# Half of the input rows and the memory tokens arrive already turned instead of being turned on TensorE

## The reference, cut to what matters

```
rmsnorm(x, g) = x * rsqrt(mean(x * x, axis=-1) + 1e-6) * g
h    = rmsnorm(x, norm_mix_g)                 # (2048, 1024)
proj = h @ w_in                               # q, k, v, pool and memory queries: 1792 columns
mkv  = rmsnorm(mem, norm_mem_g) @ w_mem_kv    # 256 memory rows
gates = sigmoid(h @ w_gate + b_gate)          # 3072 columns
merged = gates[0]*(y_attn @ Wa) + gates[1]*(y_pool @ Wp) + gates[2]*(y_mem @ Wm)
x = x + merged @ w_out
x = x + relu(rmsnorm(x, norm_mlp_g) @ w_up)**2 @ w_down
out = rmsnorm(x, norm_final_g)
```

## Time and profile before

| | us |
|---|---|
| median of three runs | 2591.36 |
| the profiled execution's own time | 2593.32 |
| its span in the trace | 2591.5 |
| TensorE busy | 2565.0 |
| VectorE busy | 1734.6 |
| ScalarE busy | 1157.6 |
| GpSimd busy | 551.3 |

### The profile page before, as it was taken

How to read it: one execution, slowest core, us unless ns; L and a number is a source line. 1 busy time by engine, 2 the same in 40 slices (tenths; PEclk the granted TensorE clock), 3 DMA queues, 4 the chain that set the end, 5 groups by cost and what they waited for, 6 DMA issues and landing times.

```text
span 2591.5 us, 33051 instructions
## 1 busy us (share of the span) xinstructions
PE 2565.0 (99%) x12065; PEld 2128.1 (82%) x12065; DVE 1734.6 (67%) x2401; ACT 1157.6 (45%) x2131; POOL 551.3 (21%) x510
## 2 busy tenths in 40 slices
PE   8999999999999999999999999999999999999998
PEld 7888888888887887888887888888888888888887
DVE  7778657666466655658778666765557566575886
ACT  6344535344344433434456455654555243342533
POOL 1455200000022152336554333000000112111100
PEclk9999999999999999999999999999999999999999
DMA  4778555666446787787797666633355585767753
GB/s 146 253 241 258 199 183 179 186 216 225 144 136 240 236 258 256 230 276 260 231 298 230 229 220 197 218 110 118 110 172 162 114 221 109 185 150 161 201 179 114
DMA packets 346764, 508.71 MB, mean 196 GB/s; under 512 B 33208, under 2 KB 213484, under 8 KB 346604
## 3 DMA queue, kind: packets, MB, share of 16 engines
q1 hardware_dynamic: 318956, 431.08, 51.5%
q0 software_dynamic: 27648, 75.51, 11.8%
HBM read 325.12 MB, written 181.40 MB: 195 GB/s over the span
## 4 chain that ended last, share of the span: by engine, by line
PE 93%; DVE 4%; issue 1%; ACT 1%; DMA 1%; POOL 0%; SPq 0%; POOLq 0%; DVEq 0%
PE ps L2416 29%; PE ps L2418 29%; PE ps L2417 29%; PE ps L2421 2%; PE ps L2693 1%; PE ps L2670 1%; PE ps L2438 1%; DVE res_lo L1653 1%; DVE s_lo L1647 1%; PE ps L2593 1%; PE ps L2621 1%; DMA res_raw<-in_w_down 0%; DMA proj_d<-c 0%; ACT scores L1123 0%; DVE res_lo L1641 0%
## 5 line engine op out<-in xcount | busy, mean ns | idle before, releaser
L2416 PE MATMUL ps<-res_hi,s_hi 128*128 128x512 f32 x3084 | 1204.3, 391 | 6.4 <-issue 1.7
L2418 PE MATMUL ps<-res_hi,s_lo 128*128 128x512 f32 x3084 | 1200.9, 389 | 0.0
L2417 PE MATMUL ps<-res_lo,s_hi 128*128 128x512 f32 x3084 | 1200.9, 389 | 0.0
L2416 PEld LDWEIGHTS ps<-res_hi,s_hi 128*128 128x128 f32 x3084 | 579.1, 188 | 130.0 <-issue 6.1
L2418 PEld LDWEIGHTS ps<-res_hi,s_lo 128*128 128x128 f32 x3084 | 579.0, 188 | 120.7
L2417 PEld LDWEIGHTS ps<-res_lo,s_hi 128*128 128x128 f32 x3084 | 579.2, 188 | 118.1
L1123 ACT ACTIVATE s_hi<-piece_f 128x512 fp32r<-128x512 f32 x436 | 274.3, 631 | 478.6 <-PE ps L2418 420.6
L1123 ACT ACTIVATE s_hi<-s_sum 128x512 fp32r<-128x512 f32 x327 | 204.1, 628 | 367.5 <-PE ps L2418 338.6
L1647 DVE TENSOR_TENSOR s_lo<-piece_f,s_hi 128x512 fp32r<-128x512 f32 x432 | 322.6, 747 | 34.5 <-ACT s_hi L1123 26.5
L1647 DVE TENSOR_TENSOR s_lo<-s_sum,s_hi 128x512 fp32r<-128x512 f32 x327 | 247.8, 758 | 87.9 <-ACT s_hi L1123 87.7
L1707 DVE TENSOR_TENSOR u<-u,ps 128x512 f32<-128x512 f32 x109 | 74.8, 686 | 294.5 <-PE ps L2418 294.4
(11 more groups left out here) (195 smaller groups left out, 2501.7 us busy)
## 6 DMA issues: line engine op xcount, KB each, us to landing
proj_d<-c SPq DMA_DIRECT2D x152, 256.0 KB, 3.3
piece_f<-in_w_up SPq DMA_DIRECT2D x32, 1024.0 KB, 6.8
up_d<-c SPq DMA_DIRECT2D x128, 256.0 KB, 3.3
piece_f<-up_d SPq DMA_DIRECT2D x32, 1024.0 KB, 7.0
piece_f<-in_w_gate SPq DMA_DIRECT2D x24, 1024.0 KB, 7.1
w_hi<-parts_d SPq DMA_DIRECT2D x48, 512.0 KB, 3.7
w_lo<-parts_d SPq DMA_DIRECT2D x48, 512.0 KB, 5.2
temp<-proj_d SPq DMA_DIRECT2D x48, 512.0 KB, 6.8
```

The lines of the kernel that those rows point to most:

```text
L2416: mm(dst, wh, xh, start=first, stop=False, skip_group_check=joins)
L2417: mm(dst, wh, xl, start=False, stop=False, skip_group_check=joins)
L2418: return mm(dst, wl, xh, start=False, stop=last, skip_group_check=joins)
```

## The change

The host gives two more inputs: the second half of x and the memory rows, laid out turned. For the five portions, TensorE's transposes and VectorE's products with the gain go away. In their place SyncE loads the turned portion into `ht` (1 MB, iteration N), ScalarE multiplies by the gain in two halves of four ACTIVATEs of 128x256 (iteration N+1), SyncE stores the 256 row factors to DRAM and loads them back, broadcast to all partitions, as `r_bc`, and GpSimd multiplies `ht` by them in four TENSOR_TENSORs (end of iteration N+1). Both halves of `ht` are stored in iteration N+2, before C22. The untouched rows are still loaded, for the sums of squares. Some semaphores are merged, with counts to match.

```diff
...
+            def load_turned(n):
+
+                if n not in NORM_AT:
                     return
...
+                if across(n):
+                    sp.wait_ge(hs_st, 64 * summed(n))
+                    for r in range(2):
+                        sp.wait_ge(ht_st[r], 16 * across(n))
+                else:
+                    sp.wait_ge(r_lo_done, PROD)
+                frm = a["mem_turned"] if n == MEM_AT else a["x_turned"][NORM_AT.index(n)]
+                sp.dma_start(ht[:], frm).then_inc(xt_ld, 16)
+
+            def store_factors(n):
...
+                sp.wait_ge(rs_pow, normed(n) + 1)
+                if across(n):
+                    sp.wait_ge(r_ld, 16 * across(n))
+                sp.dma_start(r_d[:], rrs[:]).then_inc(r_st, 16)
+
+            def load_factors(n):
...
+                sp.wait_ge(r_st, 16 * (across(n) + 1))
+                if across(n):
+                    sp.wait_ge(ht_done, 2 * across(n))
+                sp.dma_start(r_bc[:].rearrange("p n i -> p (n i)"),
+                             r_d.rearrange("n i -> (n i)").rearrange("(o n) -> o n", o=1).broadcast_to([P, 2 * P])).then_inc(r_ld, 16)
+
+            def store_turned(n):
...
+                sp.wait_ge(ht_done, 2 * across(n) + 2)
+                for r in range(2):
+                    if n == MEM_AT:
+                        sp.dma_start(mt_v[:, :, r * P:(r + 1) * P], ht[:, r]).then_inc(ht_st[r], 16)
+                    else:
+                        store_across(ha_v, n, r)
...
+                    load_turned(n)
                     if 0 <= n - SPLIT_AT < PARTS:
...
                         if across(n + 1):
-                            sp.wait_ge(xt_rdy, 2 * across(n + 1))
+                            sp.wait_ge(rs_sum, 4 * normed(n + 1))
                         load_rows(n + 1)
...
+                    store_factors(n - 1)
+                    store_turned(n - 2)
                     store_tile(n, 0, C22, 1, 1)
...
                     store_tile(n, 1, C11, 0, 0)
+                    load_factors(n - 1)
...
+            def turned_weighted(n, half):
+
+                if n not in NORM_AT:
+                    return
+                act.wait_ge(xt_ld, 16 * (across(n) + 1))
+                g0 = PM_MEM if n == MEM_AT else PM_MIX
+                for k in range(4 * half, 4 * half + 4):
+                    last = op(ht[:, :, k, :], ht[:, :, k, :], ACT.Copy, scale=par[:, g0 + k:g0 + k + 1])
+                last.then_inc(xn_done, 1)
...
             def norm_tiles(n):
 
-                if not hosts(n):
+                if not out_job(n):
...
                         norm_tiles(n - 1)
+                    turned_weighted(n - 1, 0)
                     if more:
                         s_split(n + 1, 2)
...
                         s_split(n + 1, 3)
+                    turned_weighted(n - 1, 1)
                     finish(n, C11, 2)
...
             def take_ht(n, r):
-                if not hosts(n):
+                if not out_job(n):
...
+                if n in NORM_AT and across(n) or n == IN_END:
+                    pool.wait_ge(r_st, 16 * across(n))
                 g_.tensor_tensor(rrs[:], rvar[:], m_half[:, 0:2], ALU.pow).then_inc(rs_pow, 1)
+
+            def turned_scaled(n):
...
+                pool.wait_ge(xn_done, 2 * across(n) + 2)
+                pool.wait_ge(r_ld, 16 * (across(n) + 1))
+                for r in range(2):
+                    by_row = r_bc[:, :, r].rearrange("p (o n) -> p o n", o=1).broadcast_to([P, 4, P])
+                    for h in range(2):
+                        half_row = ht[:, r, 4 * h:4 * h + 4, :]
+                        last = g_.tensor_tensor(half_row, half_row, by_row, ALU.mult)
+                    last.then_inc(ht_done, 1)
...
                         weight_sums(SUMS_AT.index(n))
+                    turned_scaled(n - 1)
...
             def rows_across(n, r):
 
-                if not hosts(n):
+                if not out_job(n):
...
```

More of the change, by code:

```diff
@@ L164, in across, with crossed @@
     return count(hosts, n)
+def crossed(n):
+    return count(out_job, n)
 def summed(n):
@@ L318, in build @@
     t1_raw = there("t1_raw", [P, 4, TB], 120)
+    r_bc = there("r_bc", [P, P, 2], 126)
     b21_raw = there("b21_raw", [P, 4, TB], 188)
@@ L394, in build @@
     setup = sem("setup")
-    ident_rdy = sem("ident_rdy")
     par_rdy = sem("par_rdy")
@@ L488, in build @@
     with_gain = sem("with_gain")
-    gf_ld = sem("gf_ld")
+    xt_ld = sem("xt_ld")
+    r_st = sem("r_st")
+    r_ld = sem("r_ld")
     def kp(w):
@@ L764, in store_tile, with store_across @@
                 sp.dma_start(to[r0:r0 + P, c0:c0 + TB], c_tile(n, which)[:]).then_inc(up_st[s], 16)
[L766 to L768 removed]
+            def load_turned(n):
+                if n not in NORM_AT:
                     return
[L770 to L774 removed]
+                if across(n):
[8 more added lines that the diff above has]
+                if n not in NORM_AT:
+                    return
+                sp.wait_ge(rs_pow, normed(n) + 1)
[3 more added lines that the diff above has]
+            def load_factors(n):
+                if n not in NORM_AT:
+                    return
[5 more added lines that the diff above has]
+            def store_turned(n):
+                if n not in NORM_AT:
+                    return
+                sp.wait_ge(ht_done, 2 * across(n) + 2)
[4 more added lines that the diff above has]
+                        store_across(ha_v, n, r)
+            def store_across(to, n, r):
+                t0 = t_at(n, r)
                 if r == 0:
@@ L778, in store_ht @@
                     sp.dma_start(to[:, 4:8, t0:t0 + P], ht[:, 1, 4:8, :]).then_inc(ht_st[1], 16)
+            def store_ht(n, r):
+                if not out_job(n):
+                    return
+                sp.wait_ge(ht_done, 2 * across(n) + r + 1)
+                store_across(ht_v, n, r)
             def store_sums(n):
@@ L2469, in rows_across @@
             def rows_across(n, r):
-                if not hosts(n):
+                if not out_job(n):
                     return
                 pe.wait_ge(xn_done, 2 * across(n) + r + 1)
-                if 2 * across(n) + r:
+                if 2 * crossed(n) + r:
                     pe.wait_ge(ht_done, 2 * across(n) + r)
@@ L2554, in pool_rows_across @@
                     last = transpose(ps[:, 6, g * P:(g + 1) * P], wp_st[:, g, :])
-                last.then_inc(wp_tr, 1)
+                last.then_inc(misc_done, 1)
             def fuse_pool(u):
@@ L2805 @@
         aps[name] = nc.dram_tensor(f"in_{name}", arrays[f"in_{name}"].shape, F32, kind="ExternalInput").ap()
+    x, mem = inputs["x"][0], inputs["mem"][0]
+    turned = {"x_turned": x[SEQ // 2:].reshape(2, 4, P, KT, P).transpose(1, 4, 0, 3, 2),
+              "mem_turned": mem.reshape(2, P, KT, P).transpose(3, 0, 2, 1)}
+    for name, laid in turned.items():
+        arrays[f"in_{name}"] = np.ascontiguousarray(laid)
+        aps[name] = nc.dram_tensor(f"in_{name}", arrays[f"in_{name}"].shape, F32, kind="ExternalInput").ap()
     out = nc.dram_tensor("out", (1, SEQ, D), F32, kind="ExternalOutput").ap()
```

39 lines of the change are left out of this document (19 added, 20 removed).

## The result

The changed kernel takes **2606.99 us** (median of 6 runs, 2601.70 to 2611.61); the kernel before, on the same chip, 2591.07 (2589.86 to 2592.15, 6 runs). The ratio is 1.0061, 95% interval 1.0044 to 1.0078: slower by 15.9 us, where the forecast was 2582.5 us, 8.9 less than before. The profiled execution took 2610.12 us, with a span of 2608.3.

A forecast was written before the change was run, and what follows sets the result against it. TensorE was taken to bound the kernel, busy 99% of the span and waiting for nobody from 70 to 345 us. Removed transposes gave -8.9, all else zero: 2591.36 to 2582.5 us, range 2580.7 to 2587.0.

The forecast's parts named there:

- What was removed: TensorE, input stage: ten groups of eight transposes at 0.89 us a group leave the chain, 8.9 us.
- the rival with 2569.6: TensorE: each of 80 transposes counts in full at 0.272 us, 21.8 us saved; chance 1%.
- What ScalarE and VectorE get: ScalarE: eight ACTIVATEs at 0.40, 3.2 us a portion, hidden by idle time; VectorE: loses 13.6 us off the path.
- VectorE is held up: VectorE stands still beside GpSimd's 25.9 us of new products, ending 12.3 us behind; at TensorE's cost 2594.8 us; chance 3%.
- The price of the parts on GpSimd and SyncE: GpSimd: 1.295 us a product, 5.2 a portion; SyncE: fifteen issues of 0.34 us, factor store and load landing in 4 each.
- the broadcast product is dear: GpSimd's product with a broadcast operand: slower by over 5.2 us from 3.7 us each, 2600.2 at 4.0; chance 5%.
- the tightest place: After portion 10, SyncE holds C22 and C11 for GpSimd; 6.9 and 6.5 us of slack remain, at worst 1.2 lost.
- the DMA queues are late: Loads for portions 4, 7, 10 each delay GpSimd's chain 4.6 us; TensorE waits 7.3 beside pieces 13, 14: 2589.8; chance 9%.
- where the queues were emptier: Argument against the late-queues rival: the turned loads come right behind the piece load, when DMA queues had less to do.
- the zero: The sum's entry for everything except the removed transposes: no gain and no loss counted.

The follow-up runs named there:

- the run with rests: Changed kernel with GpSimd's ten weight-sum sets spread over pieces 2 to 15 instead of 2 to 11: 2582.36 us, ratio 0.9966.
- the control without the change: Kernel before, with its weight sums spread over pieces 2 to 15 in the same way: 2591.30 us, ratio 1.0001.
- order-only kernel: Changed kernel with SyncE's factor, scaled-portion and block-sum transfers moved behind the store of C21: median 2600.37 us, ratio 1.0024; profiled again 2585.05.

## Why the prediction was wrong, point by point

**What was removed: right.** 8.9 us for ten groups; the run with rests is 8.7 under the kernel before, the control without the change 0.3 over it. A transpose costs the chain the distance of starts, not its 272 ns: the rival with 2569.6 would have asked for 22 us in the run where nothing waits. The page "TensorE: Matmul & The Clock Gate" of the Trainium skill (Part 4) gives about 275 ns for such a transpose in one kernel, in a sentence on bf16; the 272 ns of an fp32 one here agree with it as the length of one, not as its price.

**What ScalarE and VectorE get: right in the place, ScalarE's size too small.** Eight ACTIVATEs of 495 ns are 3.96 us a portion, over the 3.2 taken and the upper bound of 3.8, and they cost nothing; the wait for the turned load was 0.4 us. The rival "VectorE is held up" shows in one row, the s_lo of 5.18 us beside the scaling of portion 7; but VectorE then waited 7.29 us for the landing all the same, and the products alone in the kernel before cost no time (2591.23).

**The price of the parts on GpSimd and SyncE: right.** A product with the repeated operand takes 1.31 us (1.295 was taken), so the rival on the other side, "the broadcast product is dear", had the right sign for a wrong reason. The 8-byte store landed in 4.1 to 6.8 us, the broadcast load in 4.2 to 6.7, inside the bounds.

**The step that failed is the tightest place**, in two terms. First, the slip of the DMA queues was entered once, as one load of 1.05 MB at 230 GB/s, 4.6 us at portion 10. I took all other landings from the kernel before. But GpSimd's sets are a chain through some twenty landings, and every later one can slip: by the tenth set it was 34 us, not 4.6. Second, the end of scaling portion 10, put at 284.6, came at 314.75, and with it everything that SyncE held. The place itself was named rightly: C22 of piece 12, held behind the finished portion, stops S4 of piece 13, and that is the second wait, 8.0 us. What was not priced at all is the same place at portion 7, where the first and longest wait is (11.2 us): the argument there was that 5.2 us of scaling fit into a wait of 8.07. They do (the load at 243.91 follows the scaling without a wait), but the set ahead of it began late, with its first sum at 231.10 instead of 209.49.

**The rival "the DMA queues are late" had the mechanism**, with waits beside pieces 13 and 14, and 9%. Its size was wrong: 7.3 us lost instead of 28.1, and the longest wait is already at piece 10. It let each load delay the chain once, by its own transfer: 13.8 us, and the loads alone did make it slip by some 10 (below). It left out that SyncE's list, held by GpSimd, can return the delay: behind a bunch GpSimd waits 9.5 us for a load of weights and 11.3 for a store, GpSimd is later, and SyncE is held longer. Two executions of the order-only kernel fit this return path, and the runs without loads or without scaling say that it takes both to start it. One argument against the rival did not hold: "where the queues were emptier". In the kernel before the DMA engines are 0.92 busy from 170 to 190 us and 0.86 from 230 to 250, where the loads for portions 7 and 10 go out, against 0.70 in the whole stretch.

**Where the zero came from.** I asked what stands behind each new wait and found room, with the release times of the kernel before, though what is waited for lies in the chain that the change loads.

**How far the parts are shown.** Worked out as above, waits for weight landings plus added busy time against the kernel before, up to the tenth set's first sum, the slip of GpSimd's landings in the profiled executions is an estimated 10 us with the loads alone, 1 with the products alone, 13 with both, 9 without the loads, 8 without the scaling, 9 and 7 with the other order, and 34 in the changed kernel. So the large slip appears only where all of them meet. That SyncE's bunches are what makes the step from 13 to 34 is argued from their landings, not shown singly.

**Still open**: how the 25 us divide between volume, scaling and order. They don't add (2.1, 0.4, both 4.7), and taking away the loads gives back 21 us, the scaling 13, the order 7 in the median. The two groups of runs in two of the experiments stay unexplained beyond the granted clock.

## What to carry to other kernels

Work that fits into an engine's wait for a landing is free only while that landing stays where it was; if the engine's list is a chain of loads and stores, price a new transfer at every landing of the chain, not once. Before a wait is put into an in-order queue, ask whether what it waits for can itself be slowed by what the queue then holds back: that would be a loop. Here the slip was some 10 us where a part of it was missing, and 34 where all parts met. Slack may be cheap to place: two pieces without a weight set gave back 20 of the 25 us.

## What was unexpected in the hardware

In this case's changed kernel a long pause of TensorE costs more than its length. After 11.6 and 8.4 us without a start the next twelve matmuls or so start 0.427 us apart instead of 0.227. The windows of the changed kernel before the first pause, right after it, a little later, and right after the second show the granted clock (the third number from the end):

```profile
230.00:241.60 11.60, 11.60 (x53) 9.61 (x52) 10.23 (x10) 4.65 (x8) 10.11 (x9) 1.00 0.68 246
253.30:258.00 4.70, 4.70 (x11) 3.73 (x12) 4.67 (x4) 1.71 (x4) 4.62 (x4) 0.50 1.10 259
258.50:265.00 6.50, 6.50 (x30) 5.37 (x29) 5.27 (x9) 4.89 (x11) 1.16 (x3) 1.00 1.05 368
321.00:326.00 5.00, 4.98 (x12) 3.94 (x13) 2.37 (x4) 1.15 (x2) 0.00 (x0) 0.50 1.03 266
```

It is 1.00 (the 2.4 GHz level) up to the first pause, 0.50 (the 1.2 GHz level) right after it, and 1.00 again in the window from 258.5. Eleven or twelve starts at 0.200 us more are 2.2 to 2.4 us; with the slower first one it is 2.5 us for the first pause and 2.7 for the second. After the two short gaps (2.42 and 1.29) the second matmul starts 0.306 after the first, and from then on they are 0.227 apart.
